# State space scan: gate difference and its minimum with zero, head by head on DVE

## What is computed

```
G = cumsum(g)                         # per head, inside the chunk
diff  = G[i] - G[j]
decay = exp(diff) where j is not after i, else 0
inner = ((C @ B.T) * decay) @ (dt * x)
state = exp(G_last) * state + B.T @ (x * dt * exp(G_last - G))
y     = inner + (C @ state) * exp(G)
```

## Time and profile before

| | us |
|---|---|
| median of 3 runs | 4800.57 |
| lowest and highest of them | 4798.05, 4803.61 |
| the execution that was profiled | 4797.95 |
| its span in the trace | 4796.1 |
| scan of group 0, in the trace | 2112.6 to 2230.9 |
| scan of group 1, in the trace | 2346.2 to 2462.1 |

### The profile page before, as it was taken

One profiled execution on the slowest core, in us unless ns is written; L12 is line 12 of the kernel. 1 busy time (PEld: TensorE's weight loads), 2 busy tenths in 40 slices (PEclk: granted clock), 3 DMA queues, 4 the chain that ended last, 5 costly groups with the idle time before them and its releaser, 6 DMA issues.

```text
span 4796.1 us, 45140 instructions
## 1 busy us (share of the span) xinstructions
PE 4370.5 (91%) x18128; PEld 3031.7 (63%) x18128; DVE 2342.6 (49%) x3763; ACT 1395.5 (29%) x2615; POOL 971.0 (20%) x746
## 2 busy tenths in 40 slices
PE   7895799998999999988889998989888888999998
PEld 3454764757788888655544455555564657888886
DVE  2768974253555663345442017563666644333334
ACT  3462221123211111432311015351454533222222
POOL 0114544121443441024341000001000011000001
PEclk9997899999999999988899999999999999999999
DMA  5112243112333431220201110011000031111111
GB/s 189 36 64 66 88 131 111 31 44 79 104 103 110 118 115 36 76 69 29 70 27 35 44 37 27 27 53 57 20 21 16 29 105 44 45 53 44 44 44 62
DMA packets 255713, 300.42 MB, mean 63 GB/s; under 512 B 19040, under 2 KB 209904, under 8 KB 254224
## 3 DMA queue, kind: packets, MB, share of 16 engines
q1 hardware_dynamic: 234976, 216.66, 14.7%
q0 software_dynamic: 17408, 75.64, 5.0%
q10 hardware_dynamic: 3120, 5.24, 0.3%
HBM read 267.42 MB, written 30.09 MB: 62 GB/s over the span
## 4 chain that ended last, share of the span: by engine, by line
PE 62%; DVE 9%; ACT 5%; POOL 1%; issue 1%; DMA 1%; POOLq 0%; DVEq 0%; ACTq 0%
PE bank L193 60%; PE bank L196 2%; DVE Mx L205 1%; ACT at21P L202 1%; ACT at20P L202 1%; ACT Mx L202 1%; DVE at21sm L223 1%; POOL sq L205 1%; DVE at20sm L223 1%; DVE x L211 0%; DMA wslot<-in_w_in 0%; DVE wfl L205 0%; DVE at11sm L223 0%; DVE at21Pl L205 0%; DVE at10sm L223 0%
## 5 line engine op out<-in xcount | busy, mean ns | idle before, releaser
L193 PE MATMUL bank<-h,wslot 128*128 128x512 f32 (+3 forms) x2096 | 896.9, 572 | 32.9 <-DMA wslot<-in_w_in 19.2
L193 PEld LDWEIGHTS bank<-h,wslot 128*128 128x128 f32 (+1 forms) x2096 | 381.8, 190 | 377.8 <-issue 360.7
L193 PE MATMUL bank<-hT,wslot 128*128 128x512 f32 (+3 forms) x1136 | 462.6, 564 | 13.7 <-DMA hT<-hspill 6.9
L193 PEld LDWEIGHTS bank<-hT,wslot 128*128 128x128 f32 (+1 forms) x1136 | 212.2, 189 | 239.1 <-issue 232.3
L193 PE MATMUL bank<-ffn1h,wfh 128*128 128x512 f32 x704 | 280.6, 399 | 10.2 <-DVE ffn1l L211 9.4
L193 PE MATMUL bank<-ffn2h,wgh 128*128 128x512 f32 x704 | 276.5, 393 | 9.6 <-DVE ffn2l L211 9.2
L211 DVE SCALAR_TENSOR_TENSOR x<-bank,mod,x 128x512 f32<-128x512 f32 x224 | 164.3, 746 | 245.0 <-PE bank L193 244.7
L193 PE MATMUL bank<-ffn1l,wfh 128*128 128x512 f32 x704 | 275.9, 392 | 0.0
L193 PE MATMUL bank<-ffn1h,wfl 128*128 128x512 f32 x704 | 275.4, 391 | 0.0
L193 PE MATMUL bank<-ffn2l,wgh 128*128 128x512 f32 x704 | 274.9, 391 | 0.0
L193 PE MATMUL bank<-ffn2h,wgl 128*128 128x512 f32 x704 | 274.7, 390 | 0.0
(11 more groups left out here) (533 smaller groups left out, 8879.5 us busy)
## 6 DMA issues: line engine op xcount, KB each, us to landing
wslot<-in_w_in SPq DMA_DIRECT2D x40, 1024.0 KB, 5.6
ffn1t<-in_w_mod POOLq DMA_DIRECT2D x64, 512.0 KB, 4.8
wslot<-in_w_ffn_in SPq DMA_DIRECT2D x44, 512.0 KB, 5.4
Mx<-acsT SPq DMA_DIRECT2D x32, 512.0 KB, 4.8
at1w<-in_ada_w POOLq DMA_DIRECT2D x24, 512.0 KB, 4.7
wslot<-in_ffn_w_gate SPq DMA_DIRECT2D x22, 512.0 KB, 4.0
wslot<-in_ffn_w_up SPq DMA_DIRECT2D x22, 512.0 KB, 5.3
wslot<-in_w_ffn_out SPq DMA_DIRECT2D x20, 512.0 KB, 5.2
```

Of the source, the lines that this page charges most:

```text
L193: return Counted() if counting[0] else self.q.matmul(o, l, r, start=start, stop=stop)
```

## The change

The difference is no longer one TENSOR_TENSOR over 128 x 1024 but eight TENSOR_SCALARs over 128 x 128, one for each head, each with the head's column of `acs` as its scalar and with two operations: subtract, then the minimum with zero. The relu on ACT goes, and the exponential reads the result with no sign. The last of the eight signals what the one signalled before. ACT has one activation less for each of the 32 items, DVE seven instructions more.

```
-                e.tensor_tensor(heads(mx), heads(mx), acs[:, j:j + 8].unsqueeze(2).to_broadcast([128, 8, 128]), OP.subtract).then_inc(st.dve("a", m), 1)
+                for h in range(8):
+                    e.tensor_scalar(tok(mx, h), tok(mx, h), acs[:, j + h:j + h + 1], 0.0, OP.subtract, OP.min).then_inc(
+                        st.dve(*(("a", m, h) if h < 7 else ("a", m))), 1)
...
-                e.activation(mx[:, :], mx[:, :], AF.Relu, scale=-1.0).then_inc(st.act("r", m), 1)
-                e.wait_ge(*st.act.after("r", m))
-                e.activation(mx[:, :], mx[:, :], AF.Exp, scale=-1.0).then_inc(st.act("m", m), 1)
+                e.activation(mx[:, :], mx[:, :], AF.Exp).then_inc(st.act("m", m), 1)
```

## The result

The changed kernel takes 4817.71 us (median of 5 runs, 4814.89 to 4830.80) against 4799.86 us before (median of 5, 4794.95 to 4803.61). The ratio of the means is 1.0042 with a 95% interval of 1.0031 to 1.0053: slower by 0.42% (the medians alone give 0.37%, 17.9 us). The profiled execution has a span of 4815.8 us, 19.7 more than before. The forecast was 4824 us, +24 by the sum of terms.

What follows compares the result with a forecast made beforehand. The prediction took PE as the bound overall and a ring of DVE, PE and POOL in the scans; +19 us at short distances, +4.4 at starts and 0 at long ones made about +24, so 4824.5 us, range 4788 to 4842.

Steps and rivals of the forecast that it cites:

- the ring DVE, PE, POOL: In both scans, engines wait for each other in a ring; the change attacks DVE's wait for ACT, 22.9 us.
- starts: Start of each group's scan: POOL has four operations ready, first inside block +2.2 us later, +4.4 us in all.
- short blocks: Inside blocks of 3.76 us; behind them DVE never waits for PE: four distances at +2.3, three at +3.3, +19 us.
- long blocks: Inside blocks of 7.06 us; behind them DVE waits for PE with about 3 us of slack, so 0 change.
- The relu: ACT's path loses 1.06 us plus hand-over per item: -12 us at short distances, -2 us at starts, if nothing else moved.
- The price of eight with POOL idle: On DVE, eight TENSOR_SCALARs cost 0.19 us each, 1.6 us for eight; 2.15 us without the double rate.
- The turns: DVE and POOL alternate, one operation each, so the eight short operations wait for POOL: about +24 us, 4824 us.
- The walk for 2136.36: Distance 2136.36 to 2147.75: six POOL operations fall into the difference, next inside block at 2150.0, +2.3 us.
- the step on long distances: Distances behind 7.06 us blocks: 0 taken, +1 us each as upper bound; wrong if those blocks move by more than that.
- B: Rival: the eight pass as a pack, POOL before or after; -12 us at short distances, 4788 us; chance 0.12.
- C: Rival: TENSOR_SCALAR with a column does not meet POOL, 2.15 us for eight; gain 10 us, 4791 us; chance 0.11.
- D: Rival: nothing measurable, loss from turns about as large as the gain; 4796 to 4808 us; chance 0.17.

Runs made afterwards that it cites:

- nomin1: Kernel before without the relu and with no minimum, difference still one TENSOR_TENSOR, exponential of a hundredth of it (output not the reference's): 4787.6 us, ratio 0.9980.
- keep_relu: Changed kernel with the relu and its wait put back on ACT, eight TENSOR_SCALARs kept: 4833.1 us, ratio 1.0077.
- nomin8: As nomin1, but the difference cut into eight TENSOR_TENSORs of 128 x 128: 4826.3 us, ratio 1.0060.
- psum_zero: Changed kernel with each of the eight a SCALAR_TENSOR_TENSOR taking zeros from PSUM as second tensor, ring of seven banks: 4781.7 us, ratio 0.9966.
- psum_both: As psum_zero, and the masked product cbm also written to PSUM, ring of six banks: 4774.5 us, ratio 0.9949.

## Why the prediction came out as it did

*What bounds the scan.* Right in the main: the ring DVE, PE, POOL held. Summed over both groups: starts +4.4 us (2.1 and 2.3; forecast 2.2 each), the 14 distances between inside blocks +18.3, and behind the last blocks -1.8, since the last of group 0 takes 5.02 us where it took 7.06. That is 20.8 us, against 23.5 by the terms. The last part the prediction didn't have, and it had all of the distances on the seven behind short blocks, which came to +15.1 (forecast 19); the seven behind long blocks came to +3.2 (forecast 0).

*The relu.* Right in kind, and a little large in size: -12 and -2 us forecast, together -14; measured -11.5 us in the scans of nomin1 (-8.8 by the medians), and 12.0 us by keep_relu.

*The price of eight with POOL idle.* 1.6 us forecast, 1.65 us measured, but the way to it was luck. The prediction took 0.26 us for each of eight operations that read PSUM and subtracted 0.07 for a double rate. The runs show that the gap has another source: TENSOR_TENSORs of the same size in SBUF, which the prediction has at the single rate, take 1.70 for eight (nomin8), 0.05 more and not 0.5, and operations that read PSUM 2.15. So at 128 columns the rate is hardly seen, and whether a TENSOR_SCALAR with a column has the double one is not shown. The estimate of 1.0 us by the Trainium skill, page "VectorE: DVE Perf Modes", section "The TRN2 errata", is too low here; its advice against small tiles would have pointed the right way, but for another reason than the one that cost the time.

*The turns.* Right in the mechanism, and it decided. The walk for 2136.36 gave six POOL operations in one difference and +2.3 us; the trace shows six, and +2.05 (11.39 to 13.44 us). The four early distances behind short blocks came to +2.0 to +2.3 us each. The three later ones, forecast at +3.3 each, came to +2.05 (2184.56, where the walk had +3.2), +1.06 and +3.6, 6.7 in all. The 3.2 us that are missing came up, by chance, at distances that had stood behind long blocks: the walk had held fixed which blocks are short. After the change they are others,

```profile
2178.45 7.06 PE L193 MATMUL bank<-xt,Mx 128*128 128x64 f32 x32 [5.93 <-DVE Mx L205]
...
2192.90 3.75 PE L193 MATMUL bank<-xt,Mx 128*128 128x64 f32 x32 [1.16 <-DVE Mx L205]
...
2208.91 7.06 PE L193 MATMUL bank<-xt,Mx 128*128 128x64 f32 x32 [8.53 <-DVE Mx L205]
...
2222.36 5.02 PE L193 MATMUL bank<-xt,Mx 128*128 128x64 f32 x32 [1.50 <-DVE Mx L205]
```

and the distance 2192.90 to 2208.91 is 16.0 us where the same one, then behind a long block, had been 13.45. That is over the 1 us that the prediction named as its sign of being wrong in the step on long distances. Of the seven, three are unchanged (11.41 twice, 13.29), three move by under 0.5 us, and this one breaks the step.

"The block of 2210.40 comes +3.7 us later" was wrong by itself: that distance grew by 1.06. The prediction has a short distance as DVE's own queue plus its waits for ACT. In this one, before the change, DVE did not wait for ACT at all but twice for POOL's H:

```profile
2200.85 0.69 DVE L205 TENSOR_TENSOR H<-bank,H 128x512 f32<-128x512 f32 x1 [1.00 <-POOL H L205]
...
2207.05 0.69 DVE L205 TENSOR_TENSOR H<-bank,H 128x512 f32<-128x512 f32 x1 [1.00 <-POOL H L205]
```

How much of the miss that wait accounts for is not shown. The close agreement of the whole sum is partly luck, as errors of 3.2 us each way cancel.

*A column as the scalar.* The prediction left open whether such a TENSOR_SCALAR meets POOL. It does, 1305 ns at most. The rule of the Trainium skill, page "SBUF — State Buffer", section "Who interferes with whom", agrees with the contact in each case that these runs touch: TENSOR_SCALAR, to which the page gives a two-port mode, yes (the changed kernel); two inputs in SBUF, yes (nomin8); one in SBUF and one in PSUM, no (psum_zero, psum_both).

*The rivals.* B, the eight pass as a pack, and C, no contact, are out by the 6.47 us. psum_zero has what C supposed, no contact at 2.15 us for eight: C's forecast was a gain of 10 us, measured are 15 by the medians and 21 in the scans. C had counted little for the turns that the difference had cost before; that this is the whole gap is not shown. D, nothing measurable, is out by the interval of the ratio.

## What to carry to other kernels

Count who shares a resource with an engine before an operation is cut into pieces: when DVE and POOL alternate, the number of DVE operations sets how often DVE stands still, and each turn costs one POOL operation (here 1.0 us), whatever DVE's piece is worth (0.2 us). A shorter path on an idle engine (ACT, 12 us here) is easily outweighed by that. Giving one input of DVE's operations a place in PSUM took the turns away (psum_both). With the relu gone as well it was worth 22 us on this kernel by the medians, of which the relu alone gives 9.

## What the runs showed of the hardware

- Eight independent DVE operations, issued back to back with no wait between them, don't hold POOL off: once POOL has work, it gets in after each, and one operation to one they alternate. POOL keeps its pace of 1.00 us, the one it has without contact (1.04 us each in psum_both). Beside such short pieces the loss is all on DVE's side; beside DVE's operations over 1024 columns POOL loses too (2.02 us).
- A DVE operation with one input in SBUF and one in PSUM runs beside POOL at no cost to either: 328 to 349 ns over 256 of them.
- The inside blocks of 3.76 and 7.06 us are the two levels of PE's clock, 2.4 and 1.2 GHz. In the changed kernel the stretches at 2138.4 and 2152.0 show it (stretch, its length, busy by engine, then the granted clock 1.00 and 0.50); ahead of the second PE had waited 5.97 us for DVE, ahead of the first 1.35 us:

```profile
2138.40:2142.00 3.60, 3.60 (x33) 3.60 (x34) 3.08 (x11) 1.06 (x1) 0.67 (x1) 1.00 0.03 7
2152.00:2158.80 6.80, 6.80 (x33) 6.80 (x34) 5.49 (x20) 1.06 (x1) 0.00 (x0) 0.50 0.00 0
```

  So a wait of PE can be followed by up to 3.3 us more in the block behind it. The wait just ahead of a block does not decide it alone. In nomin1 the same wait stands ahead of a block of either kind:

```profile
2142.95 3.76 PE L193 MATMUL bank<-xt,Mx 128*128 128x64 f32 x32 [1.98 <-DVE Mx L205]
...
2371.49 6.95 PE L193 MATMUL bank<-xt,Mx 128*128 128x64 f32 x32 [1.98 <-DVE Mx L205]
```

  In both kernels the two kinds mostly alternate, and the change moved which blocks are short. That long blocks give DVE time to catch up would explain the alternation; it was not tested.
